# Second attention of a two-layer encoder trunk: weight loads and low parts one at a time, fills one step later, late units in places of their own, three tiles squared inside the loop

## What is computed

```python
qb = q.reshape(bsz, nc, CHUNK, C_KV_HEADS, grp, HEAD_DIM)
kb, vb = band(k), band(v)        # each chunk of 64 with the chunk before it
logits = jnp.einsum('bnqkgd,bnskd->bnkgqs', qb, kb) * HEAD_DIM ** -0.5 + bias
p = softmax(concatenate([logits, sink]))[..., :-1]
out = jnp.einsum('bnkgqs,bnskd->bnqkgd', p, vb)
mix = out.reshape(bsz, s_len, C_HEADS * HEAD_DIM) @ w_out
h = h + rms_norm(mix, g[1])
f = sqrelu_mlp(rms_norm(h, g[2]), ffn_w1[i], ffn_w2[i])
h = h + rms_norm(f, g[3])
```

## Time and profile before

| what | value |
|---|---|
| median of 3 runs | 2552.21 us (2549.1 to 2555.14) |
| the profiled execution | 2550.85 us |
| its span, first to last instruction | 2548.8 us |
| TensorE busy | 2417.9 us (95%) |
| VectorE, ScalarE, GpSimd busy | 1707.7, 1183.6, 1472.0 us |
| mean granted clock of TensorE | 0.981 |

### The profile page before, as it was taken

How to read it: one execution, slowest core, us unless ns; L and a number is a source line. 1 busy time by engine, 2 the same in 40 slices (tenths; PEclk the granted TensorE clock), 3 DMA queues, 4 the chain that set the end, 5 groups by cost and what they waited for, 6 DMA issues and landing times.

```text
span 2548.8 us, 34095 instructions
## 1 busy us (share of the span) xinstructions
PE 2417.9 (95%) x11680; PEld 1989.2 (78%) x11680; DVE 1707.7 (67%) x2857; ACT 1183.6 (46%) x2025; POOL 1472.0 (58%) x815
## 2 busy tenths in 40 slices
PE   7899999898998999999999999979889999999997
PEld 5689888776776778888778887868777888778886
DVE  5469999667775486555666686157778656566676
ACT  5442533556664274444343335255566444434331
POOL 2111578645553149877778643346645878577961
PEclk9899999899999999999999999989999999999999
DMA  5390644733555624555645445655553554754343
GB/s 149 64 130 26 133 99 134 239 102 98 157 135 166 215 79 141 165 152 158 228 163 165 141 134 154 154 145 137 150 160 100 170 148 141 258 184 140 115 141 132
DMA packets 330517, 369.64 MB, mean 145 GB/s; under 512 B 14003, under 2 KB 229587, under 8 KB 328325
## 3 DMA queue, kind: packets, MB, share of 16 engines
q1 hardware_dynamic: 321748, 351.96, 47.3%
q10 hardware_dynamic: 8352, 15.21, 2.1%
q0 software_dynamic: 272, 0.62, 0.1%
...
## 4 chain that ended last, share of the span: by engine, by line
PE 80%; DVE 7%; ACT 5%; issue 3%; DMA 3%; POOL 2%; SPq 0%; DVEq 0%; ACTq 0%; POOLq 0%
PE ps L461 75%; PE ps L2703 2%; PE ps L2777 1%; DMA h_operand_raw<-h_operand_scratch 1%; ACT relu_scores L1532 1%; DVE masks L2093 1%; POOL w_split L416 1%; DVE acc L1923 1%; DVE probs_T L2262 1%; ACT junk L1366 1%; DVE logits L2227 1%; PE ps L2712 1%; PE ps L578 1%; DMA hidden<-cat_scratch 1%; PE ps L2787 0%
## 5 line engine op out<-in xcount | busy, mean ns | idle before, releaser
L461 PE MATMUL ps<-xn_T,w_split 128*128 128x512 f32 (+1 forms) x2928 | 676.4, 390 | 2.2 <-ACT x_sums L1409 2.0
L461 PEld LDWEIGHTS ps<-xn_T,w_split 128*128 128x128 f32 (+1 forms) x2928 | 546.3, 187 | 119.9 <-DVE xn_T L2026 2.5
L461 PE MATMUL ps<-w_operand,h_operand 128*128 128x512 f32 x2016 | 464.1, 392 | 12.9 <-DVE acc L2499 6.0
L416 POOL TENSOR_TENSOR w_split<-w_raw,w_split 128x1024 fp32r<-128x1024 f32 x76 | 193.7, 2560 | 454.2 <-ACT w_split L409 453.8
L461 PEld LDWEIGHTS ps<-w_operand,h_operand 128*128 128x128 f32 x2016 | 381.1, 189 | 95.9 <-issue 11.5
L1280 POOL TENSOR_TENSOR w_split<-w_raw,w_split 128x512 fp32r<-128x512 f32 x168 | 244.3, 1466 | 101.7 <-ACT w_split L1787 100.3
L461 PE MATMUL ps<-x_sums_high,w_split 128*128 128x512 f32 x896 | 284.9, 389 | 0.0
L1312 POOL TENSOR_TENSOR w_operand<-w_block,w_operand 128x2048 fp32r<-128x2048 f32 x42 | 207.7, 4946 | 112.5 <-ACT w_operand L1807 112.3
L2501 DVE TENSOR_TENSOR acc<-acc,ps 128x512 f32<-128x512 f32 x288 | 185.3, 681 | 120.0 <-PE ps L461 119.4
L461 PE MATMUL ps<-w_split,unit_tile 128*128 128x512 f32 x720 | 200.0, 412 | 19.9 <-issue 10.5
L1794 ACT ACTIVATE h_operand<-h_operand_raw 128x2048 fp32r<-128x2048 f32 (+1 forms) x56 | 95.3, 1702 | 261.7 <-DMA h_operand_raw<-h_operand_scratch 261.7
...
## 6 DMA issues: line engine op xcount, KB each, us to landing
...
q_scratch<-q_split SPq DMA_DIRECT2D x128, 128.0 KB, 2.6
cat_scratch<-attn_out_split SPq DMA_DIRECT2D x128, 128.0 KB, 2.6
...
```

The source lines that it names most:

```text
L416: nc.gpsimd.tensor_tensor(whl[:, n0 % 4, 1, :], wraw[:, n0 % 4, :], whl[:, n0 % 4, 0, :].bitcast(F32), ALU.subtract).then_inc(w_lo, 1)
L461: return nc.tensor.matmul(out_ap, stat, mov, start=start, stop=stop)
```

## The change

- The loads of `T_O1 + 4` to 7 move from step 1 to steps 8, 10, 12 and 14, one each, those of `T_F1` to `T_F1 + 2` from step 25 to steps 26, 28 and 30, the one of `T_F1 + 3` behind everything else of `sp_attn1`.
- Fills 32 to 47 are in steps 6 to 21, fills 48 to 55 in steps 24 to 31.
- VectorE makes the four low parts one at a time between the logits: in step 22 behind the third logits, in step 23 behind the first and the third, in step 24 behind the first. ScalarE's high parts stay in steps 21 and 22.
- Unit 4 gets a buffer of its own and is loaded in step 27; unit 5 goes to the other half of `fu1` and is loaded in step 29, once fill 53 is taken. As unit 4 lies where the normed rows will be written, `scale` waits for its two products.
- ScalarE squares blocks 0, 1 and 2 of `acc` at the end of steps 26, 28 and 30, rather than behind the attention.

```diff
--- before.py
+++ after.py
@@ -92,7 +92,8 @@
 WIDTH1 = [P if b == 0 else P + CHUNK for b in range(NB)]
 STEP1 = [(2 * kv + e, b) for kv in range(2) for b in range(NB) for e in range(2)]
 T_BASE1 = [sum(1 if b == 0 else 2 for _, b in STEP1[:g]) for g in range(HG * NB + 1)]
-FILL1 = {g: [32 + g - 5] if 5 <= g < 21 else [48 + g - 23] if 23 <= g < 31 else [] for g in range(HG * NB)}
+FILL1 = {g: [32 + g - 6] if 6 <= g < 22 else [48 + g - 24] if 24 <= g else [] for g in range(HG * NB)}
+LOWS1 = {(22, 2): T_O1 + 4, (23, 0): T_O1 + 5, (23, 2): T_O1 + 6, (24, 0): T_O1 + 7}
 X0 = [sum(KEYS0[b % NB] for b in range(g)) for g in range(HG * NB + 1)]
 BANK_USES = [u for g in range(HG * NB) for u in [("t", X0[g] + st) for st in range(KEYS0[g % NB])] + [("d", g)]]
 LEAD0 = 2
@@ -262,6 +263,7 @@
     fu0 = at("unit_tile", [P, 2, 4, 2, P], F32R, D0 + 68 * K)
     fu1 = at("unit_tile1", [P, 2, 4, 2, P], F32R, D0 + 20 * K)
     late = at("late_units", [P, 2, 4, 2, P], F32R, D0)
+    unit_4 = at("unit_tile_4", [P, 4, 2, P], F32R, XT0 + 41 * K)
     part = at("part_sum", [P, 2, 512], F32, D0 + 76 * K)
     first_part = at("first_part", [P, 2, 512], F32, D0 + 80 * K)
     half_sum = at("half_sum", [P, 4, D], F32, D0 + 68 * K)
@@ -338,6 +340,7 @@
     od_ld = [S(f"half_sum_ld{t}") for t in range(NB)]
     cat_ld = [S("cat_ld0"), S("cat_ld1")]
     cat_first, cat_rest = S("cat_last_first"), S("cat_last_rest")
+    u4_ld = S("unit_tile_4_ld")
     w1_ld = [S("w1_ld_even"), S("w1_ld_odd")]
     w1_sum, w1_hi, w1_lo = S("x_and_w1_sums"), S("w1_high"), S("w1_low")
     x_hi, x_lo = S("x_raw_high_first_tiles"), S("x_sums_low")
@@ -807,9 +810,12 @@
 
             sp.wait_ge(fo_free, k + 1)
             u = k // 2 + 2
-            if k % 2 and u < 30:
+            if k % 2 and u < 28:
                 step_pair_spilled(2 * (u - 16))
                 fill_units(sp, 1, u)
+            if k == 53:
+                step_pair_spilled(27)
+                unit_tiles(sp, fu1[:, 0], 1, 5, fu_ld[0])
 
         def spill(g):
 
@@ -824,10 +830,17 @@
                 after_fill(k)
             spill(g)
             if g == 1:
-                for n in range(T_O1 + 4, T_O1 + 8):
-                    load_tile(sp, n, tile_src(n))
                 for e in range(2):
                     sp.wait_ge(q_sp[e], 1024)
+            if g in (8, 10, 12, 14):
+                n = T_O1 + 4 + (g - 8) // 2
+                load_tile(sp, n, tile_src(n))
+            if g in (26, 28, 30):
+                n = T_F1 + (g - 26) // 2
+                load_tile(sp, n, tile_src(n))
+            if g == 27:
+                step_pair_spilled(25)
+                unit_tiles(sp, unit_4[:], 1, 4, u4_ld)
             if g in (1, 3):
                 step_pair_spilled(g)
                 fill_units(sp, 1, 16 + g // 2)
@@ -836,9 +849,6 @@
                 sp.wait_ge(l1_free, 64)
                 for t in range(2):
                     load_h(sp, 3, t)
-            if g == 25:
-                for n in range(T_F1, T_F1 + 4):
-                    load_tile(sp, n, tile_src(n))
             if g == 29:
                 step_pair_spilled(g)
                 unit_tiles(sp, late[:, 0], 1, 6, cat_first)
@@ -847,6 +857,7 @@
                     load_h(sp, 3, t)
         step_pair_spilled(HG * NB - 1)
         unit_tiles(sp, late[:, 1], 1, 7, cat_rest)
+        load_tile(sp, T_F1 + 3, tile_src(T_F1 + 3))
 
     def toeplitz(l, h, n):
 
@@ -1391,6 +1402,7 @@
             if s == 3 and t == 0:
                 for e in range(2):
                     act.wait_ge(o_sp[e], 16 + 1024)
+                act.wait_ge(b_full, B_O1 + 2)
             nc.scalar.activation(xn[:, 0, :, t * P:(t + 1) * P], acc[:, t, :].rearrange("p (k m) -> p k m", k=KT), ACT.Copy,
                                  scale=rsb[:, t:t + 1]).then_inc(n_x, 1)
 
@@ -1428,11 +1440,17 @@
             split_hi(act, 2)
             split_hi(act, 3)
 
+        def first_tiles(g):
+            if g in (26, 28, 30):
+                square_a((g - 26) // 2, 3)
+
         def norm(s, between=None):
-            square_a(0, s)
-            square_a(1, s)
+            if s != 3:
+                square_a(0, s)
+                square_a(1, s)
             root_a(0, 2)
-            square_a(2, s)
+            if s != 3:
+                square_a(2, s)
             square_a(3, s)
             root_a(2, 2)
             square_b(0, s)
@@ -1652,7 +1670,7 @@
                 last = nc.scalar.activation(vodd[half * HD:(half + 1) * HD, :, 4 * k:4 * k + 4, 0, :], tiles[HD:P], ACT.Copy)
             last.then_inc(a_hi, 1)
         split_hi(act, T_O1 + 3)
-        act_attn1(act)
+        act_attn1(act, first_tiles)
         norm(3)
         act_ffn(act, LAYERS[1], xn_high, xn_raw)
         norm_end(4)
@@ -1713,7 +1731,7 @@
                 split_hi(act, n)
                 split_hi(act, n + 1)
 
-    def act_attn1(act):
+    def act_attn1(act, first_tiles):
 
         for s_ in range(2):
             act.wait_ge(q_sp[s_], 1024)
@@ -1755,6 +1773,7 @@
                     split_hi(act, n)
             if g + 5 < HG * NB:
                 load_q(act, qst1, g + 5, q_tile1(g + 5))
+            first_tiles(g)
 
     def act_ffn(act, L, xn_high, xn_raw):
 
@@ -2352,8 +2371,10 @@
             s = g % 2
             q = T_BASE1[g]
             todo = list(range(4)) if g + 1 < HG * NB else []
-            for _ in range(LEAD1 if todo else 0):
-                logits(g + 1, todo.pop(0))
+            for j in todo:
+                logits(g + 1, j)
+                if (g, j) in LOWS1:
+                    weight_low(LOWS1[g, j])
             dve.wait_ge(e1_ok, 4 * g + 4)
             nc.vector.reciprocal(rinv[:, s, :], rsum[:, s, :]).then_inc(r1_ok, 1)
             if g:
@@ -2361,12 +2382,7 @@
             if STEP1[g][1]:
                 probs_low(pS1[HD:P, s, :], ps[0:HD, 4 + q % 2, :], pS1[0:HD, s, :], q)
                 q += 1
-            for j in todo:
-                logits(g + 1, j)
             probs_low(pL1[:, s, 1, :], ps[:, 4 + q % 2, :], pL1[:, s, 0, :], q)
-            if g in (22, 23):
-                for n in range(T_O1 + 4 + 2 * (g - 22), T_O1 + 6 + 2 * (g - 22)):
-                    weight_low(n)
             for k in FILL1[g]:
                 take_fill(k)
         output(HG * NB - 1)
@@ -2850,7 +2866,7 @@
 
         def unit(t, half, f, j, start, stop):
 
-            units = fu1[:, t % 2] if t < 6 else late[:, t % 2]
+            units = unit_4 if t == 4 else fu1[:, 0] if t == 5 else late[:, t % 2]
             n, o = T_O1 + 4 + j, ps[:, 4 + f % 4, :]
             wh = whl[:, n % 4, 0, half * 512:(half + 1) * 512]
             wl = whl[:, n % 4, 1, half * 512:(half + 1) * 512]
@@ -2860,8 +2876,10 @@
 
         def loaded(t):
 
-            if t < 6:
-                pe.wait_ge(fu_ld[t % 2], 32 * 15)
+            if t == 4:
+                pe.wait_ge(u4_ld, 32)
+            elif t == 5:
+                pe.wait_ge(fu_ld[0], 32 * 15)
             else:
                 pe.wait_ge(cat_rest if t == 7 else cat_first, 32 + 32)
```

## The result

The changed kernel took 2531.25 us in the median (four runs, 2524.78 to 2535.06), the kernel before 2552.11 us beside it (four runs, 2549.1 to 2555.14). The ratio is 0.9916 (95% interval 0.9892 to 0.994). The change made the kernel faster by 21 us.

The account below looks back on a forecast made before the run. Filled steps were taken as bound by TensorE, with only idle, low-clock stretches to win back. Terms -13.9 - 6.3 - 1.6 + 2.4 - 1.2 = -20.6 us, from the median 2552.2, gave 2531.6 us; 8-in-10 range 2525.5 to 2540.

Parts of the forecast that it names:

- parts 1 and 2: Steps 5 and 6 with the first fill, 13.9 us less; steps 21 to 25 with the low parts, 6.3 us less.
- parts 3 and 4: Last fills: 1.6 us less in step 29, 2.4 more for step 31's fill; output projection and norm: 1.2 less.
- The first fill: Steps 5 and 6: without loads ahead and one step later, the fill finds its unit just in time; 13.9 us less.
- Rival (a): First unit still late, by 5.8 us plus 2 us of low clock: saving 12.8 us, time 2539.4 us; chance 0.1.
- The low parts: Steps 21 to 25: low parts one at a time and later fills take 24.6 us against 30.97; 6.3 us less.
- clean sum: Steps 21 to 24 without low-part or clock costs: 5.69 us for step 21, 13.13 us for steps 22 to 24.
- Rival (b): Steps 21 to 25: low parts become the wait, saving there 2.3 us, total 16.6, time 2535.6 us; chance 0.12.
- The last fills: Attention's end: spread loads and a unit issued earlier remove step 29's wait, 1.6 us less; step 31's fill costs 2.4.
- Output projection and norm: Behind the attention: VectorE's first scaling starts 1.9 us earlier, next stage's products 1.2 us earlier, bounds 0 and 2.5.
- Rival (c): Output projection and norm: the chain gains as much as TensorE's wait was, 8 us instead of 1.2; 2524.8 us; chance 0.04.
- Rival (d): TensorE stays at 1.2 GHz after steps 22 to 24, filled steps not raising it; up to 2577 us; chance 0.02.
- a filled step beyond 5.8 us: Sign of being wrong, in the attention's steps: a step with a fill growing beyond 5.8 us, against 5.69 us before.

Follow-up runs that it names:

- f0: The changed kernel without an edit, timed and profiled again: 2531.59 us, ratio 0.9930 to the kernel before.
- e6: The changed kernel with the four loads of the next stage (`T_F1` to `T_F1 + 3`) together in step 25 again: 2531.01 us.
- e7: The changed kernel with VectorE's inverse of the sums taken ahead of the low part in steps 22 to 24: 2532.73 us.
- e1: The kernel before with only the four weight loads of step 1 moved to steps 8, 10, 12 and 14: 2542.03 us.
- e2: The kernel before with only the fills one step later, loads together in step 1 and low parts in pairs: 2541.47 us.
- e3: The changed kernel with the low parts made in pairs again at the ends of steps 22 and 23: 2530.63 us.
- e10: The changed kernel with each of the four weight low parts cut to 8 of its 1024 columns: 2529.86 us.
- e11: The changed kernel with the third low part moved from step 23 to filled step 24, the fourth behind the third logits there: 2530.36 us.
- e4: The changed kernel with the three squares back behind the attention: 2537.01 us.
- e5: The changed kernel with units 4 and 5 again in the halves of `fu1`, unit 5 loaded once fill 55 is taken: 2535.11 us.

## Why the prediction was right

The predicted 2531.6 us stand beside measured 2531.25 and 2531.59. The saving was forecast at 20.6 us; the medians give 20.9 and, with f0, 17.4 (the kernel before took 2548.94 us beside it). Some of the closeness is luck: the two profiles gained 20.9 and 19.0 us at P1, where the sum ends, and step 5 to P2 alone lies between 215.8 us (e6) and 218.8 us (f0) with almost the same code. Two step prices in the sum were wrong and cancel (2). In the first profile parts 1 and 2 gave 0.65 and 0.2 us less than forecast, parts 3 and 4 0.9 and 0.3 more.

1. **The first fill: right.** 13.25 us gone for 13.9 forecast. The missing 0.65 us is in step 6, which I priced as a filled step among filled ones: its fill starts 2.33 us into it (1697.02 to 1699.35), at a bare step's pace, that of step 7 1.59 us (1703.46 to 1705.05), so step 6 takes 6.44 us and not 5.69. The landing came out nearly as worked out: no idle in most profiles, but 0.42 and 0.92 us in f0 and e7, where the fill began 4.5 and 4.9 us behind the end of the issue and not 3.7. e1 and e2 show that both edits were needed. Rival (a), a wait of 5.8 us, fell; e2 is what it would have looked like. Spreading the four loads cost nothing in steps 7 to 21 (79.69 for 79.66 us).
2. **The low parts: right in sum, with two wrong prices that cancel.** 24.84 us for 24.6; f0 had 25.86, so 5.1 us less than before where I had 6.3. The clean sum took every bare step at 3.72 us and every filled one at 5.69, but a step's length depends on the one ahead of it. A bare step behind a filled one took 2.98 us: step 21 of the kernel before ran from 1792.32 to the row shown here, and step 22 of e2 and e3 was as long.

```profile
1795.30 0.89 PE L461 MATMUL ps<-k_split,q_tile 128*128 128x192 f32 x6
```

A filled step behind a bare one took 6.44 us, as step 6 did (6.58 for step 24 of e10). 5.69 + 2.98 + 3.72 + 6.44 = 18.83 is the 5.69 + 13.13 = 18.82 of the prediction by luck. Above it the changed kernel has 4.71 us in the bare steps 22 and 23, where I had 4.8 for three low parts (they took 4.95), and 1.29 us in step 24. The clock cost 14.26 - 13.01 = 1.25 us (TensorE's busy time in steps 22 to 24, the changed kernel less e11) for 1.0, and 15.30 - 13.01 = 2.3 in f0. The idle was not spread as I had written (1.5 to 2 us each): one piece was 3.28 us, since two low parts stand in step 23, and e11 shows that this is where the clock goes. Rival (b) had 2.3 us for this part; it fell.
3. **The last fills: right in direction of each term, wrong cause, 0.9 us off.** Step 29 lost 1.8 us for 1.6. "Spread over steps 26, 28, 30 and the end, with the unit issued three steps ahead, the wait goes" names two causes, and e6 leaves only the second. Steps 30 and 31 cost 1.75 us more for 2.4, less even than the lower bound that I gave (1.97), which was again a filled step less a bare one at 3.72. Together the part cost 0.1 us less where I had 0.8 us more. The squares inside the loop cost nothing: steps 25 to T are 40.19 us with them and 40.14 without (e4).
4. **Output projection and norm: right size, stage cut too early.** T to P1 fell by 1.5 us (1.2 in f0) for 1.2; VectorE's first scaling began at 1850.19, T + 2.0, for T + 1.9; TensorE's idle before the transpositions was 1.78 + 3.24 = 5.0 us for "some 5", though only the 3.24 are the wait for the normed rows that I described. What failed is where the sum stops. "From there the chain's own work is the same" holds of the work and not of its neighbours: VectorE and GpSimd meet there, and P1 to P2 took between 0.2 us less and 2.5 us more than before (28.6 to 31.3 against 28.81). Whether the change makes the long outcomes likelier is open: the kernel before has one profile. Rival (c), 8 us, fell: the chain on VectorE and ScalarE is the bound. e4 and e5 divide the part otherwise than I did: 0.5 to 0.7 us for the squares, and 2.7 to 2.95 for the places, of which some 1.9 may only undo what the moved loads would have cost.
5. **Rival (d), the clock, fell.** Filled steps behind filled ones stayed at 5.7 us; steps 7 to 21 and 25 to 29 (22.79 us, before 22.80) are unchanged. Yet one sign that the prediction gave for being wrong appeared, a filled step beyond 5.8 us: steps 6 and 24 took 6.44 and 7.73. The sign was drawn too tight, as it left out that a filled step behind a bare one is longer, and part 2 itself had the clock's 1.0 us behind the thin steps.

**What stays open.** Why some executions fall to the lower clock earlier after the same idle; what decides between VectorE and GpSimd when they meet (one kernel has 31.24 and 29.47 us, another 28.60 and 31.27); and where ahead of the second attention the spread of 12.7 us in step 5's start arises. A kernel with e11's place and e6's loads together was not tried.
